# Down products of a feed-forward layer: two accumulations of 256 columns in one bank in place of one of 512

## The chip, the cores and the metric

The kernel runs on one core of one Trainium2 chip. The metric is the device time of one execution in microseconds; the median of three runs before the change is 2027.84 us (2025.33 to 2028.24). TensorE does the matrix products and reads its results out into accumulation banks of 512 float32 columns on 128 partitions; VectorE (DVE), ScalarE (ACT) and GpSimd (POOL) do the rest, SyncE (SP) starts most transfers.

## The reference, cut to what matters

The kernel computes one layer of a streaming encoder for 1152 tokens (1024 of a prompt and 8 x 16 of samples) and a model width of 1024: token mixing (a state-space half and a differential-attention half), cross-attention into 256 memory tokens, and a dense gated feed-forward network (FFN). The change touches only the last:

```python
hn = rms_norm(h, g_pre_ffn)
f = (jax.nn.silu(hn @ w_gate) * (hn @ w_up)) @ w_down     # hidden 2816
h = h + rms_norm(f, g_post_ffn)
```

All products are float32 in and out. The kernel splits each operand into a high part, rounded to the format that TensorE takes in one pass (fp32r), and a low part, the rest, and adds three products: high by high, high by low, low by high.

## The kernel before, in words

`three(out, pairs, release)` (lines 217 to 227) is the helper for every such product. For each pair of operands it issues three matmuls into one bank: line 222 (high, high), line 225 (high, low) and line 226 (low, high). The first of each matmul's operands is the stationary one (128 x 128, loaded by a weight load of its own ahead of every matmul, the PEld rows), the second is the moving one, whose columns are streamed. In the profile's rows the moving tile stands first: `bank<-w_hi,hid_h 128*128 128x512` moves 512 columns of w_hi past the stationary hid_h. `release` names pairs whose first matmul tells POOL that a weight slot has become free (semaphore w_used).

Weights come as items of 128 x 1024: SP loads them into w_raw, POOL splits each into w_hi and w_lo (`split`, lines 578 and 580), four slots of each. They are waited for with w_ready.

Where `three` is used, with the number of moving columns:

- token-major projections (`tm_chunk`), 256 columns of w past stationary NH/NL, 8 pairs (24 matmuls) to a bank; between them memory projections (`mem_unit`), 256 columns as well
- output projections (`join_unit`), 256 columns of w past stationary YH/NL, and later OH/OL, 24 matmuls to a bank
- scores of the cross-attention (`x_scores`), 256 columns of mkh/mkl past stationary QXh/QXl: two groups of 6 matmuls, one into each half of one bank
- linear projections (`lin_unit`) and the FFN's gate and up products (`up_unit`): 384 columns of the activations past stationary w, 24 matmuls to a bank
- the FFN's down products (`down_unit`): 512 columns of w past a stationary tile of the hidden, 2 pairs (6 matmuls) to a bank

The FFN goes through the hidden in 11 groups of 256. One group is 12 up units (288 matmuls), then SiLU on ACT, product, rounding and rest on DVE and ACT (`hid_raw`, `hid_high`, `hid_low`) into hid_h and hid_l, all of them two buffers; the down products of a group run after the up products of the next. A down is 18 units (9 token tiles x 2 column halves of the output), 108 matmuls. Unit q takes bank 6 + q % 2, waits until DVE has added what was in it (f_de) and, when its last matmul ends, gives f_dn; DVE's `add_down` (line 2053) adds the whole bank to ACC. On TensorE two groups are one pass of a hardware loop of 5 passes (`Fori`); the last down stands behind the loop, uses 6 banks, and is followed tile by tile by the final norm: ACT squares (line 244), DVE scales (`last_scale`, line 2059), POOL adds the residual, SP stores.

Of the kernel before, what the change touches and what calls it, by code (L numbers as in the profile page):

```python
# [65 lines left out]
def build(nc, x_in, mem_in, wall, wdt, consts, vecs, gains, rows, kc, vc, h0, sconv, cmk, cmv,  # L66
          y_o, k_o, v_o, ssm_o, conv_o, mk_o, mv_o, zs_d, q_d, h_d):
    with ExitStack() as ctx:
# [28 lines left out]
        whi, wlo = [T[f"w_hi{i}"] for i in range(4)], [T[f"w_lo{i}"] for i in range(4)]  # L97
# [71 lines left out]
        g = T.__getitem__  # L169
# [47 lines left out]
        def three(out, pairs, release=()):  # L217


            n = len(pairs)  # L220
            for i, (ah, al, bh, bl) in enumerate(pairs):
                m = mm(out, ah, bh, start=(i == 0), stop=False)  # L222
                if i in release:
                    m.then_inc(w_used, 1)
                mm(out, ah, bl, start=False, stop=False)  # L225
                m = mm(out, al, bh, start=False, stop=(i == n - 1))  # L226
            return m
# [5 lines left out]
        def tok(t):  # L233
            return slice(P * t, P * t + P)
# [380 lines left out]
        def _(pe):  # L615
# [50 lines left out]
            for kind in range(4):  # L666
                tm_chunk(kind, 0)
                tm_chunk(kind, 1)
                if kind == 2:
# [10 lines left out]
                    for t in range(NT):  # L680
                        m = nc.tensor.transpose(B[7][:, SH * t:SH * t + SH], g("dtr")[0:SH, tok(t)], ident[0:SH, 0:SH])
# [3 lines left out]
            with pe.Fori(0, KT // 4) as i:  # L685
                for s in range(4):
                    pe.wait_ge(w_ready, I_XB + s + 1 + 4 * i)
                    for c in range(CH):
# [4 lines left out]
                              release=((0,) if c == 0 else ())).then_inc(xb_mm, 1)  # L693
# [70 lines left out]
            for t in range(NT):  # L764
# [6 lines left out]
                for h in range(SH):  # L771
                    m = mm(B[6][:, SP_ * h:SP_ * h + SP_], g("MT")[:, h, :], g("xdt")[:, SP_ * h:SP_ * h + SP_],  # L772
                           start=True, stop=True)
# [4 lines left out]
                if t < NT - 1:  # L778
                    for gr in range(2):
                        m = mm(B[7][:, 256 * gr:256 * gr + 256], g("Btm")[:, gr, :], g("xdd")[:, 256 * gr:256 * gr + 256],  # L780
                               start=True, stop=True)
# [20 lines left out]
            for t in range(NT):  # L802
                if t < DB:
                    new_state(t)
                for w in range(2):
# [5 lines left out]
                    for h in range(H):  # L811
                        m = nc.tensor.transpose(B[6 + w][:, tok(h)], g(f"qkr{t % 2}")[:, w, tok(h)], ident)
# [91 lines left out]
            for u in range(U):  # L904
# [19 lines left out]
                if u == 17:  # L924
                    pe.wait_ge(a_yte, 3)
                    for h in range(H):
                        m = nc.tensor.transpose(B[7][:, tok(h)], g("oTs")[:, h, :], ident)
                    m.then_inc(b_sum, 1)
                if u == 18:
                    pe.wait_ge(b_p, DB + 1)  # L930
                    for h in range(H):
                        m = nc.tensor.transpose(B[7][:, tok(h)], g("QTs")[:, h, :], ident)
# [168 lines left out]
            def down(par, n0, s0, ready, hid):  # L1101
                pe.wait_ge(w_ready, ready)
                pe.wait_ge(f_hl, hid)
                for q in range(2 * NT):
                    pe.wait_ge(f_de, n0 + q + 1)
                    down_unit(par, s0, q, B[6 + q % 2],
                              ((0,) if q == 0 else (1,) if q == 2 * NT - 1 else ())).then_inc(f_dn, 1)

            def down_unit(par, s0, q, out, release=()):

                t, half = q // 2, slice(512 * (q % 2), 512 * (q % 2) + 512)
                return three(out, [(g(f"hid_h{par}{f}")[:, tok(t)], g(f"hid_l{par}{f}")[:, tok(t)],
                                    whi[(s0 + f) % 4][:, half], wlo[(s0 + f) % 4][:, half]) for f in range(2)], release)

            for n in range(WOVEN, 4 * NT):
                join_unit(pe, 1, I_WX, n, OH, OL)
# [20 lines left out]
            for q in range(2 * NT):  # L1137
                if q >= 6:
                    pe.wait_ge(f_de, 2 + last + q - 5)
                down_unit(0, 0, q, B[q % 6]).then_inc(f_dn, 1)  # L1140
# [1038 lines left out]
```

## Time and profile before

| | |
|---|---|
| median of 3 runs | 2027.84 us (2025.33 to 2028.24) |
| profiled execution, its own time | 2031.52 us |
| its span, first to last instruction | 2029.7 us |
| TensorE matmul busy (PE) | 1885.5 us, 93%, 12283 matmuls |
| TensorE weight load busy (PEld) | 1761.2 us, 87% |
| VectorE / ScalarE / GpSimd busy | 40% / 26% / 25% |
| mean granted TensorE clock | 0.955 |

The busy time of TensorE is the time in which some matmul is in flight; consecutive matmuls overlap, so a row's duration (0.39 us for 512 columns) is longer than what one costs in a stream. What one costs is the distance from its start to the start of the next. Starts are given to 0.01 us, so the distance is read from the first and the last of many.

### The profile page before, as it was taken

Reading aid. Unit: us, or ns where it says so; the run is one execution under the profiler, and the core shown is the slowest. Engines: PE = TensorE matmul, PEld = TensorE weight load, DVE = VectorE, ACT = ScalarE, POOL = GpSimd, SP = SyncE. Lnnn points to the kernel's source line nnn. Section 1 sums busy time; section 2 is a strip of 40 time slices with the busy share of each in tenths; the row PEclk is TensorE's granted clock in tenths of the full one; section 3 lists DMA queues with packets and bytes.
Section 4 is the critical chain, followed back from the end, with each engine's and each line's share of the span. In section 5 each row is a group of like instructions: output and inputs, shape, how many; then the busy total and the mean of one; then the engine's idle time right before and its main releaser. Section 6 shows DMA issues by size and latency. Waiting matters only on the chain.

```text
span 2029.7 us, 29875 instructions
## 1 busy us (share of the span) xinstructions
PE 1885.5 (93%) x12283; PEld 1761.2 (87%) x12283; DVE 816.2 (40%) x1633; ACT 523.1 (26%) x1279; POOL 508.0 (25%) x299
## 2 busy tenths in 40 slices
PE   7999999878677789989999999999999999999996
PEld 6999899767456669989988989999999999999995
DVE  5354116585665662361453361312322322322327
ACT  5200112265355663242343241010010010000002
POOL 3444442131000001212200312421421421421323
PEclk9999999997777889999999999999999999999998
DMA  5333331200530021121264321110110110110132
GB/s 211 111 117 111 103 133 43 101 27 21 194 106 8 1 93 64 70 108 52 84 229 153 112 99 42 53 52 21 55 48 21 62 41 21 62 41 21 62 124 93
DMA packets 56246, 160.99 MB, mean 79 GB/s; under 512 B 4176, under 2 KB 13904, under 8 KB 55888
## 3 DMA queue, kind: packets, MB, share of 16 engines
q1 hardware_dynamic: 35296, 117.13, 16.7%
q10 hardware_dynamic: 20848, 42.45, 5.9%
q8 instruction: 70, 1.15, 0.2%
q14 instruction: 32, 0.26, 0.0%
HBM read 131.41 MB, written 28.16 MB: 79 GB/s over the span
## 4 chain that ended last, share of the span: by engine, by line
PE 80%; DVE 10%; ACT 5%; issue 4%; DMA 1%; POOL 0%; ACTq 0%; SPq 0%; DVEq 0%; POOLq 0%
PE bank L222 23%; PE bank L225 23%; PE bank L226 23%; DVE at_sm L1830 1%; PE bank L995 1%; DVE H L347 1%; DVE ACC L2059 1%; PE bank L851 1%; PE bank L260 1%; PE bank L772 1%; DVE MT L1771 1%; DVE E L1764 1%; PE bank L744 1%; PE bank L840 1%; PE bank L893 1%
## 5 line engine op out<-in xcount | busy, mean ns | idle before, releaser
L578 POOL CAST w_hi<-w_raw 128x1024 fp32r<-128x1024 f32 x130 | 140.8, 1083 | 1371.2 <-PE bank L222 1205.5
L222 PE MATMUL bank<-OH,w_hi 128*128 128x384 f32 x1056 | 355.3, 336 | 0.0
L226 PE MATMUL bank<-OH,w_lo 128*128 128x384 f32 x1056 | 355.0, 336 | 0.0
L225 PE MATMUL bank<-OL,w_hi 128*128 128x384 f32 x1056 | 354.9, 336 | 0.0
L580 POOL TENSOR_TENSOR w_lo<-w_raw,w_hi 128x1024 fp32r<-128x1024 f32 x130 | 321.8, 2475 | 10.4
L226 PE MATMUL bank<-w_hi,NL 128*128 128x256 f32 x864 | 242.5, 281 | 0.0
L2039 DVE TENSOR_TENSOR hr<-sg,bank 128x384 f32<-128x384 f32 x66 | 36.5, 554 | 431.8 <-PE bank L226 431.8
L225 PEld LDWEIGHTS bank<-OL,w_hi 128*128 128x128 f32 x1056 | 198.6, 188 | 0.4
L222 PEld LDWEIGHTS bank<-OH,w_hi 128*128 128x128 f32 x1056 | 198.6, 188 | 0.4
L226 PEld LDWEIGHTS bank<-OH,w_lo 128*128 128x128 f32 x1056 | 198.6, 188 | 0.0
L2053 DVE TENSOR_TENSOR ACC<-ACC,bank 128x512 f32<-128x512 f32 x180 | 122.7, 685 | 109.5 <-PE bank L226 109.5
L226 PEld LDWEIGHTS bank<-w_hi,NL 128*128 128x128 f32 x864 | 164.6, 190 | 0.0
L222 PE MATMUL bank<-w_hi,NH 128*128 128x256 f32 x576 | 161.2, 280 | 0.0
L225 PE MATMUL bank<-w_lo,NH 128*128 128x256 f32 x576 | 160.2, 278 | 0.0
L225 PE MATMUL bank<-w_lo,hid_h 128*128 128x512 f32 x396 | 156.7, 396 | 0.0
L226 PE MATMUL bank<-w_hi,hid_l 128*128 128x512 f32 x396 | 156.7, 396 | 0.0
L222 PE MATMUL bank<-w_hi,hid_h 128*128 128x512 f32 x396 | 156.5, 395 | 0.0
L1604 ACT ACTIVATE sg<-bank 128x384 f32<-128x384 f32 x66 | 32.4, 490 | 416.8 <-PE bank L226 416.8
L225 PE MATMUL bank<-NL,w_hi 128*128 128x384 f32 x384 | 129.1, 336 | 0.0
L222 PEld LDWEIGHTS bank<-w_hi,NH 128*128 128x128 f32 x576 | 109.2, 190 | 0.0
L225 PEld LDWEIGHTS bank<-w_lo,NH 128*128 128x128 f32 x576 | 108.9, 189 | 0.0
L1613 ACT ACTIVATE hid_h<-hr 128x384 fp32r<-128x384 f32 x66 | 34.7, 525 | 278.8 <-DVE hr L2039 278.8
(343 smaller groups left out, 3722.2 us busy)
## 6 DMA issues: line engine op xcount, KB each, us to landing
w_raw<-in_wall SPq DMA_DIRECT2D x130, 512.0 KB, 3.3
scratch_h<-H ACTq DMA_DIRECT2D x6, 1536.0 KB, 5.3
MIX<-in_cmk SPq DMA_DIRECT2D x8, 1024.0 KB, 5.3
cV<-in_cmv SPq DMA_DIRECT2D x8, 1024.0 KB, 5.2
H<-in_x SPq DMA_DIRECT2D x1, 4608.0 KB, 17.4
H<-scratch_h SPq DMA_DIRECT2D x1, 4608.0 KB, 16.0
Hback<-scratch_h ACTq DMA_DIRECT2D x1, 4608.0 KB, 14.0
out_y<-Hback SPq DMA_DIRECT2D x9, 512.0 KB, 2.6
```

The lines of the kernel that those rows point to most:

```text
L222: m = mm(out, ah, bh, start=(i == 0), stop=False)
L225: mm(out, ah, bl, start=False, stop=False)
L226: m = mm(out, al, bh, start=False, stop=(i == n - 1))
L260: m = nc.tensor.transpose(turn_bank(z, j)[:, tok(i)], src[:, tok(4 * j + i)], ident)
L347: STT(out=res[:, t, :], in0=mix[:, t, :], scalar=col(S_V, n), in1=res[:, t, :], op0=ALU.mult, op1=ALU.add).then_inc(j_res, 1)
L578: pool.tensor_copy(whi[s][:], raw[s % 2][:]).then_inc(w_hi, 1)
L580: pool.tensor_tensor(wlo[s][:], raw[s % 2][:], whi[s][:].bitcast(F32), ALU.subtract).then_inc(w_ready, 1)
L744: m = mm(B[5][:, P * j + DS * b:P * j + DS * b + DS], g("h0t")[:, b, tok(j)], XC[:, 6 + j // 2, lo:lo + DS], start=True, stop=True)
L1604: act_f(g(f"sg{n % 2}")[:], B[2 * (n % 3)][:, 0:NC], ACT.Silu).then_inc(f_sg, 1)
L1613: act_f(g(f"hid_h{gi % 2}{f}")[:, cs(c)], g(f"hr{n % 2}")[:], ACT.Copy).then_inc(f_hh, 1)
L2039: TT(g(f"hr{n % 2}")[:], g(f"sg{n % 2}")[:], B[2 * (n % 3) + 1][:, 0:NC], ALU.mult).then_inc(f_hr, 1)
L2053: TT(a, a, bank_[:, :], ALU.add).then_inc(f_de, 1)
```

## The change

A down unit keeps its bank, its operands, its waits and its one signal f_dn. In place of 6 matmuls of 512 columns it issues two accumulation groups of 6 matmuls of 256 columns, the first into columns 0 to 255 of the bank, the second into 256 to 511, each with the two pairs. The weight-slot release moves to the second group. DVE still adds 512 columns at a time.

```diff
             def down_unit(par, s0, q, out, release=()):
 
-                t, half = q // 2, slice(512 * (q % 2), 512 * (q % 2) + 512)
-                return three(out, [(g(f"hid_h{par}{f}")[:, tok(t)], g(f"hid_l{par}{f}")[:, tok(t)],
-                                    whi[(s0 + f) % 4][:, half], wlo[(s0 + f) % 4][:, half]) for f in range(2)], release)
+                t = q // 2
+                for w0 in (0, 256):
+                    part = slice(512 * (q % 2) + w0, 512 * (q % 2) + w0 + 256)
+                    m = three(out[:, w0:w0 + 256],
+                              [(g(f"hid_h{par}{f}")[:, tok(t)], g(f"hid_l{par}{f}")[:, tok(t)],
+                                whi[(s0 + f) % 4][:, part], wlo[(s0 + f) % 4][:, part]) for f in range(2)],
+                              release if w0 else ())
+                return m
```

## Rows read from the trace of the kernel before

**Rows 1.** The page's part 1 and TensorE's lines of part 2 (40 slices, tenths).
```profile
PE 1885.5 (93%) x12283; PEld 1761.2 (87%) x12283; DVE 816.2 (40%) x1633; ACT 523.1 (26%) x1279; POOL 508.0 (25%) x299
PE   7999999878677789989999999999999999999996
PEclk9999999997777889999999999999999999999998
```

**Rows 2.** Page, part 4: shares of the chain that ended last, by engine.
```profile
PE 80%; DVE 10%; ACT 5%; issue 4%; DMA 1%; POOL 0%; ACTq 0%; SPq 0%; DVEq 0%; POOLq 0%
```

**Rows 3.** Groups by form, down matmuls: source line, engine, tiles, shape, count, busy us, mean ns.
```profile
L222 PE MATMUL bank<-w_hi,hid_h 128*128 128x512 f32 x396 | 156.5, 395 | 0.0
```

**Rows 4.** Timeline, TensorE, one down and its neighbours: start us, duration us, line, tiles.
```profile
1362.20 0.34 PE L226 MATMUL bank<-OH,w_lo 128*128 128x384 f32 x1
1362.38 0.39 PE L222 MATMUL bank<-w_hi,hid_h 128*128 128x512 f32 x1
...
1387.33 0.40 PE L226 MATMUL bank<-w_hi,hid_l 128*128 128x512 f32 x1
1387.57 0.34 PE L222 MATMUL bank<-OH,w_hi 128*128 128x384 f32 x1
...
1462.68 0.34 PE L222 MATMUL bank<-OH,w_hi 128*128 128x384 f32 x1
```

**Rows 5.** Timeline, TensorE, token-major projections: 168 matmuls, then 72.
```profile
138.25 0.28 PE L222 MATMUL bank<-w_hi,NH 128*128 128x256 f32 x1
...
157.29 0.28 PE L222 MATMUL bank<-w_hi,NH 128*128 128x256 f32 x1
...
165.78 0.28 PE L222 MATMUL bank<-w_hi,NH 128*128 128x256 f32 x1
```

**Rows 6.** Timeline, TensorE, first output projection, steady part: 638 matmuls.
```profile
779.77 0.28 PE L222 MATMUL bank<-w_hi,YH 128*128 128x256 f32 x1
...
854.92 0.29 PE L226 MATMUL bank<-w_hi,NL 128*128 128x256 f32 x1
```

**Rows 7.** Timeline, TensorE, cross-attention scores: 12 matmuls behind others, 10 after a pause.
```profile
936.05 0.34 PE L226 MATMUL bank<-YH,w_lo 128*128 128x384 f32 x1
936.23 0.29 PE L222 MATMUL bank<-mkh,QXh 128*128 128x256 f32 x1
...
937.67 0.33 PE L222 MATMUL bank<-YH,w_hi 128*128 128x384 f32 x1
...
1024.46 0.28 PE L225 MATMUL bank<-mkl,QXh 128*128 128x256 f32 x1
...
1025.64 0.28 PE L226 MATMUL bank<-mkh,QXl 128*128 128x256 f32 x1
```

**Rows 8.** Busy time by stretch: stretch, length, PE, PEld, DVE, ACT, POOL (instructions), clock, DMA.
```profile
218.00:283.00 65.00, 65.00 (x575) 65.00 (x575) 4.33 (x13) 12.43 (x28) 27.33 (x17) 1.00 0.23 76
1312.50:1362.20 49.70, 49.70 (x289) 49.70 (x287) 6.26 (x11) 5.57 (x11) 17.15 (x10) 1.00 0.13 43
1363.00:1387.00 24.00, 24.00 (x104) 19.32 (x104) 12.28 (x19) 0.53 (x1) 3.53 (x2) 1.00 0.13 44
```

**Rows 9.** Timeline, VectorE in the same down; in brackets the idle time before and its releaser.
```profile
1366.77 0.69 DVE L2053 TENSOR_TENSOR ACC<-ACC,bank 128x512 f32<-128x512 f32 x1 [0.71 <-PE bank L226]
1368.17 0.69 DVE L2053 TENSOR_TENSOR ACC<-ACC,bank 128x512 f32<-128x512 f32 x1 [0.71 <-PE bank L226]
```

**Rows 10.** Timeline, GpSimd around the same down.
```profile
1362.90 1.04 POOL L578 CAST w_hi<-w_raw 128x1024 fp32r<-128x1024 f32 x1 [0.69 <-PE bank L222]
1364.02 2.59 POOL L580 TENSOR_TENSOR w_lo<-w_raw,w_hi 128x1024 fp32r<-128x1024 f32 x1
1387.40 1.04 POOL L578 CAST w_hi<-w_raw 128x1024 fp32r<-128x1024 f32 x1 [20.78 <-PE bank L222]
1388.52 2.40 POOL L580 TENSOR_TENSOR w_lo<-w_raw,w_hi 128x1024 fp32r<-128x1024 f32 x1
```

**Rows 11.** Chain that ended last, in order of time, around the last down: start us, us, what.
```profile
1991.22 0.25 PE bank L226
1991.50 0.70 DVE ACC L2053
1992.28 1.15 ACT jk L244 x2
1993.45 1.28 ACT L245
...
2025.10 1.23 DVE Hback L2081
```

## The prediction

> **What bounds the kernel now.** I read the page's busy shares and slices first: TensorE is busy 93% of the span, and from the slice at about 1200 us to the last but one it stands at nine tenths in every slice, at the full clock [rows 1]. The shares of the chain that ended last say the same from the other side: 80% of it is TensorE, 10% DVE [rows 2]. So in the FFN, where the change lies, the question is what one matmul costs in a stream, and nothing else unless something begins to make TensorE wait. The groups by form give 396 matmuls of each of the three kinds of down matmul and a mean of 395 ns [rows 3], but that is a length in a pipeline, not a cost. The timeline gives the cost: from the first matmul of one down to the first up matmul behind it 1387.57 - 1362.38 = 25.19 us for 108 matmuls, 233.3 ns each, and the following down ends at 1462.68, 75.11 us later, for 288 up and 108 down matmuls; 75.11 - 25.19 = 49.92 us is 173.3 ns for each up matmul of 384 columns, so there is no gap anywhere in a period, the loop's jump back included [rows 4]. The stretches confirm it: PE is busy 49.70 of 49.70 us and 24.00 of 24.00 us, clock 1.00, that is the upper of the two levels, 2.4 GHz [rows 8].
>
> **What the change removes and adds.** It removes 6 matmuls of 512 columns and 6 weight loads in each of 11 x 18 units, and adds 12 matmuls of 256 columns and 12 weight loads. The columns streamed are the same. What decides is whether two matmuls of 256 cost more or less than one of 512, 466.7 ns for two and 233.3 for one. I count in threes, because `three` issues threes: one triple of 512 costs 700.0 ns (3 x 233.3, rows 4), and two triples of 256 take its place.
>
> How many of them set the end: 10 downs in the loop hold 10 x 18 x 2 = 360 triples. Of the last down only the start counts. The chain in order of time leaves TensorE at 1991.22 with the second unit and from there runs through DVE and ACT to the end, 2025.10 + 1.23 us [rows 11]; so two units, 4 triples, make 364.
>
> The trace has the new matmul (256 moving columns, fp32r, a new stationary tile each time, clock 1.00) in several stages, and it does not have one price there:
>
> - 168 matmuls of the token-major projections take 157.29 - 138.25 = 19.04 us, 113.3 ns each, 340.0 ns a triple [rows 5]
> - the next 72 of the same line, the same shape and the same stage take 165.78 - 157.29 = 8.49 us, 117.9 ns each, 353.8 a triple [rows 5]
> - 638 matmuls of the output projection take 75.15 us, 117.8 each, 353.4 a triple [rows 6]
> - the scores, which have the new code's very form (two groups of 6, one in each half of a bank, entered from a stream of 384), take 1.44 us for 12, 120.0 each, 360.0 a triple; another ten of them take 1.18 us, 118.0 each, 354.0 a triple [rows 7]
>
> Half of 700.0 is 350.0 ns, so the break-even of 116.7 ns a matmul lies between the levels. In terms of the kernel:
>
> - at 340.0: 2 x 340.0 - 700.0 = -20 ns, x 364 = -7.3 us
> - at 353.4: 2 x 353.4 - 700.0 = +6.8 ns, x 364 = +2.5 us
> - at 360.0: +20 ns, x 364 = +7.3 us
>
> These are the two ends and the middle. I take the middle one. The reason to stay away from the low end: the operands and the shape do not fix the level, since rows 5 hold both levels in one stage, and the level then lasts for whole units; the low level stands only in the token-major stage, while each later stage of 256 columns is at 117.8 to 120.0. The reason not to take the high end although the scores have the nearest form: they show 118.0 as well as 120.0, and their moving tiles are other ones, whereas the long streams that move w, as the down does, stand at 113.3 or 117.8. What I think limits a matmul of 256 is the weight load in front of it: in the stretch of 256 columns the weight-load side is busy 65.00 of 65.00 us, in the down only 19.32 of 24.00 [rows 8]. (That alone proves nothing: it is busy 49.70 of 49.70 us beside 384 columns too, which show one price everywhere.) With 512 columns a load has 233 ns to hide in and with 256 about 117, so the gain of a shorter matmul is there only if the load just fits.
>
> The Trainium skill, "TensorE: Matmul & The Clock Gate", section "Back-to-back issue gap", has a rule that speaks against the change: a warm matmul costs its columns at 2.4 GHz plus a fixed 2.5 ns, so each matmul more costs 2.5 ns. By that, an estimate from that page, 1092 more matmuls would add 2.7 us; rows 4 don't agree with its 215.8 ns for 512 columns, they have 233.3, and rows 5 have 113.3 where it gives 109.2. It would leave the forecast where it is.
>
> **What lies beside.** DVE adds a bank in 0.69 us and then waits 0.71 us for TensorE [rows 9]; a unit becomes 12 x 117.8 = 1.41 us instead of 1.40 (1.36 or 1.44 at the ends), so the wait f_de still finds the bank free, two units back. Nothing is added on DVE. No wait is added on TensorE; queued behind it would be only its own matmuls. The release moves: in unit 0 by six matmuls of 256, 6 x 117.8 = 0.71 us later, so the cast at 1362.90 and the rest until 1366.61 end at about 1367.3; that item is first needed by the next up at 1387.57, 20 us later. In the last unit the release comes three matmuls before the end as before, now 0.35 us before it instead of 0.70. The cast at 1387.40 starts 0.35 us later and its rest ends at 1391.3 instead of 1390.92 [rows 10]; the up unit that reads this slot is the third, 2 x 24 x 173.3 ns = 8.3 us behind 1387.57. Both cost nothing; were that cover gone, it would be 0.35 us a period, 3.5 us in all. SP's loads follow POOL's splits by the same 0.35 to 0.71 us. The loop's body holds more instructions, at a rate (a load and a matmul every 113 to 118 ns) that rows 5 and 6 show TensorE being fed without a gap, though outside a loop.
>
> **The sum.** The profiled execution took 2031.52 us, 1.82 more than its span, and 3.68 more than the median of the runs. 2031.52 + 2.5 = 2034.0 for such an execution, and against the median 2027.84 + 2.5 = 2030.3 us. I count below 0.2%, 4.1 us, as no change: about what a measurement of this kernel can tell.
>
> **Rivals.**
>
> The load just fits (faster). The down falls into the state of most of rows 5, 340.0 ns a triple: -7.3 us, 2020.5 us. For it: the down's 512-column triples come in a steady stream without a pause, they move w as rows 5 do, and a unit entered from the 384-column stream has its loads well ahead. Against it: the scores are entered from such a stream too and are not at this level [rows 7]. Chance 0.33.
>
> The load does not fit (slower). Each short group of 6 behaves like the scores at 936.23, 120.0 ns from the first matmul on [rows 7]: +7.3 us, 2035.1 us. It decides as soon as the mean is over 118.6 ns: 4.1 us over 2184 matmuls of 256 is 1.9 ns above 116.7. For it: the same form of code, two groups and two halves of a bank, with the boundary between the groups included in the 1.44 us. Against it: the 118.0 of the later scores and all the streams that move w. Chance 0.29, which takes in 0.03 for a pause at the loop's jump now that the body is longer, of which no row shows a price.
>
> The change does not do what it says: none that I see, since each half has its own first and last matmul and DVE reads the bank after the last.
>
> Forecast, 117.8 ns or a mixture of levels from down to down: chance 0.38.
>
> **How the numbers follow.** Faster by over 0.2% is the first rival, 0.33; slower by over 0.2% is the second, 0.29; within 0.2% is the forecast, 0.38. Cases of both signs hold most of the chance, so the range must reach to both ends: 2027.84 - 7.3 and + 7.3, and some 0.7 us for the scatter of the medians: 2019.8 to 2035.8. The forecast's own range is 2027.5 to 2032, mixtures taken in.
>
> **What would show it.** Between the first down matmul and the next up matmul, 216 matmuls of 256: 25.4 us by the forecast, 24.5 if the load fits, 25.9 if it doesn't, against 25.19. The up products should stay at 49.9 us a period, DVE's wait before an add at about 0.7 us, and the tail from TensorE's last link to the end at its 35 us. A down with a level that changes within it would give a mixture. The prediction would be wrong in kind if TensorE idled at the start of a down or of an up, or if the period changed outside the down.

## The result and the profile after the change

The changed kernel takes 2042.6 us, median of 4 runs (2039.7 to 2046.48), against 2027.26 us of 4 runs of the kernel before on the same chip (2025.33 to 2028.24). The ratio is 1.0070, 95% interval 1.0056 to 1.0084: slower by 0.7%, some 14 us. The forecast was 2030.3 us, no change; the time lies outside the range (2019.8 to 2035.8). The rival on the slower side had the sign, but neither the size nor, as will be seen, the cause.

The profiled execution of the changed kernel took 2041.20 us, its span is 2039.3 us. The page's busy shares and slices, and the instruction queue's line (packets, MB, share), which for the kernel before reads 70 packets, 1.15 MB, 0.2%:

```profile
PE 1881.9 (92%) x13471; PEld 1807.8 (89%) x13471; DVE 818.1 (40%) x1633; ACT 523.0 (26%) x1279; POOL 509.1 (25%) x299
...
PEclk9999999997776989999999999999999999999998
...
q8 instruction: 113, 1.85, 0.4%
```

TensorE is busy for 3.6 us less than before and the span is 9.6 us longer [rows 1]: the loss isn't in the price of a matmul, it is for the most part idle time. The weight loads are busy for 46.6 us more, since there are more of them, DVE and POOL for 1 to 2 us more; what stands out is the transfer of instructions, 113 packets in place of 70. The waits of TensorE in the FFN (tile, line <- what ended them: total us, times, longest) name two kinds, and the kernel before has none there:

```profile
PE bank L222 <- issue: 7.9, 4, 2.2
PE bank L222 <- DVE ACC L2058: 2.1, 9, 0.2
PE bank L222 <- DVE ACC L2056: 0.2, 1, 0.2
```

**The four waits for nothing.** "issue" is time for which the profile shows no releaser. The timeline of TensorE puts the four at the jump of the loop, between the last down matmul of a pass and the first up matmul of the next, of which there are four in five passes:

```profile
1384.93 0.28 PE L226 MATMUL bank<-w_hi,hid_l 128*128 128x256 f32 x1
1387.40 0.44 PE L222 MATMUL bank<-OH,w_hi 128*128 128x384 f32 x1 [2.19 <-issue]
1387.68 0.34 PE L225 MATMUL bank<-OL,w_hi 128*128 128x384 f32 x1
```

From start to start it is 2.47 us where 0.12 us would be the matmul's own cost. And behind two of the four the clock falls; it isn't the length of the pause that decides, since these two idled for 1.95 and 1.88 us and the other two for 2.19 and 1.91. The stretches (columns as in rows 8): the pause itself, then 3.9 us behind another jump at the mean clock 0.57, that is for the most part at the lower of the two levels, 1.2 GHz; then the same length behind a jump where it stays up. Thirteen matmuls where the other has 23:

```profile
1384.93:1387.40 2.47, 0.28 (x3) 0.08 (x2) 0.69 (x1) 0.00 (x0) 2.21 (x2) 1.00 0.00 0
1692.75:1696.68 3.93, 3.93 (x13) 3.93 (x14) 0.00 (x0) 0.00 (x0) 3.85 (x3) 0.57 0.33 117
1539.64:1543.60 3.96, 3.96 (x23) 3.96 (x24) 0.00 (x0) 0.00 (x0) 3.88 (x3) 1.00 0.33 98
```

**The ten waits for DVE.** They stand at the third unit of each of the ten downs of the loop (the last down, with its six banks, has none by this view). The timeline of one down, all engines:

```profile
1437.43 0.28 PE L222 MATMUL bank<-w_hi,hid_h 128*128 128x256 f32 x1
...
1438.55 1.04 POOL L578 CAST w_hi<-w_raw 128x1024 fp32r<-128x1024 f32 x1 [1.29 <-PE bank L222]
...
1438.83 1.17 DVE L2049 TENSOR_TENSOR hid_l<-hr,hid_h 128x384 fp32r<-128x384 f32 x1 [0.59 <-ACT hid_h L1618]
...
1439.92 1.27 DVE L2058 TENSOR_TENSOR ACC<-ACC,bank 128x512 f32<-128x512 f32 x2
...
1440.13 0.28 PE L226 MATMUL bank<-w_hi,hid_l 128*128 128x256 f32 x1
...
1440.65 0.39 PE L222 MATMUL bank<-w_hi,hid_h 128*128 128x256 f32 x1 [0.23 <-DVE ACC L2058]
1440.88 0.28 PE L225 MATMUL bank<-w_lo,hid_h 128*128 128x256 f32 x1
```

TensorE's 24 matmuls of the first two units are through at 1440.13 + 0.12, and unit 2 starts at 1440.65: 0.52 us from start to start, 0.40 more than a matmul's own (the wait that the view counts, 0.23, is shorter, since the matmul before is still in flight for part of it), and the matmul behind it comes another 0.11 us late, 0.23 us after it in place of 0.12: some 0.5 us a down. It needs the bank that DVE's first add empties (the row of 1.27 us holds two adds of 0.68 us, so the first ends at 1440.60), and that add is late because the subtraction ahead of it on DVE, hid_low, takes 1.17 us. In the kernel before, the subtraction of a down takes 0.57 us, and the first add, of 0.67 us, follows at once:

```profile
1363.78 0.57 DVE L2044 TENSOR_TENSOR hid_l<-hr,hid_h 128x384 fp32r<-128x384 f32 x1 [0.59 <-ACT hid_h L1613]
...
1364.28 0.67 DVE L2053 TENSOR_TENSOR ACC<-ACC,bank 128x512 f32<-128x512 f32 x1
```

The difference is POOL's cast. Before, it starts 0.52 us into the down (1362.90 - 1362.38, rows 4 and 10) and the subtraction starts 1.40 us into it, when the cast is nearly done; after, the cast starts 1.12 us into the down, and the subtraction runs beside it. The cast has moved because the change has moved the release of unit 0 into the second half.

**Where 12.8 us went.** I take the FFN from its first down matmul to the end of the span: 2029.7 - 1287.26 = 742.44 us before, 2039.3 - 1284.07 = 755.23 us after, 12.8 us more. (What stands ahead of it, which the change doesn't touch, was 3.2 us shorter in this execution, which leaves the 9.6 us of the span.) By parts, each against 25.19 us a down and 49.93 us the ups of a group:

| part of the FFN | after | difference |
|---|---|---|
| 5 downs in the middle of the body | 25.11 us each | -0.4 us |
| 4 downs ahead of the jump, pause included | 28.29, 27.18, 28.04, 27.16 us | +9.9 us |
| the 12 up units behind each of the 4 jumps | 50.03, 50.03, 51.60, 51.59 us | +3.5 us |
| from the tenth down, with the last one right behind it, to the end | 66.14 us | -0.3 us |

With the pauses left out, eight of the ten downs of the loop cost nothing: 24 matmuls at 117.8 ns, the 0.5 us at unit 2, then the rest at 113.3 to 113.4 ns. The other two, both ahead of a jump, stay at 117.8 ns behind the wait and take 25.9 us, 0.7 more than before. Both stretches of the down above, and the whole down:

```profile
1437.43:1440.65 3.22, 2.99 (x25) 2.78 (x24) 2.37 (x4) 0.53 (x1) 2.02 (x2) 1.00 0.44 163
1440.65:1462.54 21.89, 21.89 (x193) 21.89 (x193) 10.85 (x16) 0.00 (x0) 1.60 (x1) 1.00 0.07 25
1437.43:1462.54 25.11, 24.88 (x218) 24.67 (x217) 13.23 (x19) 0.53 (x1) 3.62 (x2) 1.00 0.12 43
```

The tail stands: TensorE's last link at 2001.04, and 34.97 us to the end of the last row of the chain, against 35.1 [rows 11].

```profile
2001.04 0.13 PE bank L226
2001.19 0.70 DVE ACC L2058
...
2034.78 1.23 DVE Hback L2086
```

### The profile page after: what moved, and what is told of

The parts are those of the page before. It is cut to its first block, busy times and chain, and to the rows that moved or that the text cites. A ratio compares the mean times of both kernels' runs of the same rounds, so it can differ in the third digit from the quotient of the medians.

```text
span 2039.3 us, 32251 instructions
## 1 busy us (share of the span) xinstructions
PE 1881.9 (92%) x13471; PEld 1807.8 (89%) x13471; DVE 818.1 (40%) x1633; ACT 523.0 (26%) x1279; POOL 509.1 (25%) x299
## 4 chain that ended last, share of the span: by engine, by line
PE 78%; DVE 12%; ACT 5%; issue 4%; DMA 1%; POOL 0%; ACTq 0%; DVEq 0%; SPq 0%; POOLq 0%
PE bank L222 23%; PE bank L226 23%; PE bank L225 23%; DVE at_sm L1835 1%; DVE H L347 1%; PE bank L995 1%; DVE ACC L2064 1%; PE bank L851 1%; PE bank L260 1%; DVE E L1769 1%; DVE ACC L2058 1%; DVE MT L1776 1%; PE bank L772 1%; PE bank L744 1%; PE bank L840 1%
## 5 line engine op out<-in xcount | busy, mean ns | idle before, releaser
L222 PE MATMUL bank<-w_hi,hid_h 128*128 128x256 f32 x792 | 220.9, 279 | 2.4 <-DVE ACC L2058 2.1
L226 PE MATMUL bank<-w_hi,hid_l 128*128 128x256 f32 x792 | 219.8, 278 | 0.0
L225 PE MATMUL bank<-w_lo,hid_h 128*128 128x256 f32 x792 | 219.8, 278 | 0.0
L222 PEld LDWEIGHTS bank<-w_hi,hid_h 128*128 128x128 f32 x792 | 149.3, 188 | 4.4 <-DVE ACC L2058 3.9
L226 PEld LDWEIGHTS bank<-w_hi,hid_l 128*128 128x128 f32 x792 | 149.0, 188 | 0.0
L225 PEld LDWEIGHTS bank<-w_lo,hid_h 128*128 128x128 f32 x792 | 148.7, 188 | 0.0
```

## The experiments

My theory after reading this profile had two parts. A: the loop's body has grown past what TensorE can jump back to without fetching it anew, and the late release is a second, smaller loss. B, its rival for the pause: the pace; 256-column matmuls ask for instructions faster than they come, and the jump, where fetching starts over, shows it first. The size of the body is counted from the program: 792 matmuls before, 1008 after, each with its weight load, and some 60 others, 1646 and 2078 instructions; the traces have 1645 and 2078 records of TensorE between two jumps.

### The two causes taken apart

**early_release**: the changed kernel, with the release of unit 0 back in its first half.

```diff
-                              release if w0 else ())
+                              release if (w0 == 0) == (q == 0) else ())
```

> The changed kernel, but unit 0 of a down releases its weight slot in its first half, as before the change. Theory: the late release let POOL's cast run into DVE's hid_low (1.17 us in place of 0.57), and the first add came so late that TensorE waited at unit 2 (0.4 to 0.5 us, 11 times). So here hid_low is 0.57 us again and there is no gap at unit 2; the pauses at the loop's jump (4 of about 2 us) stay. The matmuls ran at 117.8 ns before that wait and mostly at 113.3 behind it; if the wait itself sets the level, all 216 stay at 117.8, 25.44 us a down in place of 25.11, and the time is 2043 to 2046 us; if they go to 113.3 without it, 2036. Rival: the wait comes from the halves themselves (the bank is filled in two groups), and then it stays, with hid_low at 0.57.

Measured 2041.56 us (4 runs, 2039.46 to 2045.27), ratio to the kernel before 1.0067 (1.0046 to 1.0088). The wait at the third unit is gone, the subtraction is back at 0.56 us beside a cast that starts 0.42 us into the down:

```profile
1435.17 0.28 PE L222 MATMUL bank<-w_hi,hid_h 128*128 128x256 f32 x1
...
1435.59 1.04 POOL L578 CAST w_hi<-w_raw 128x1024 fp32r<-128x1024 f32 x1 [0.58 <-PE bank L222]
...
1436.58 0.56 DVE L2049 TENSOR_TENSOR hid_l<-hr,hid_h 128x384 fp32r<-128x384 f32 x1 [0.60 <-ACT hid_h L1618]
...
1460.61 0.34 PE L222 MATMUL bank<-OH,w_hi 128*128 128x384 f32 x1
```

Yet the down is longer than with the wait, 1460.61 - 1435.17 = 25.44 us against 25.11: all 216 matmuls now run at 117.8 ns, in all eleven downs. The wait had been followed by the low level, and what the mend gave back the level took. The pauses at the jump stay, and are all that TensorE waits for in the FFN:

```profile
PE bank L222 <- issue: 7.8, 4, 2.2
```

**unrolled**: the changed kernel with the five passes written out.

```diff
-            with pe.Fori(0, (NG - 1) // 2) as i:
+            for i in range((NG - 1) // 2):
```

> The changed kernel with the FFN's hardware loop on TensorE written out in full (5 passes, no jump). Theory: the body with 216 more matmuls and as many weight loads no longer stays in the instruction store and has to be fetched again at each jump back: 4 pauses of about 2 us (7.9 us of idle in all) and, behind two of them, the lower clock for about 4 us (1.8 us each). Without a jump these go: 2042.6 - 7.9 - 3.6 = 2031 us, and the waits at unit 2 stay. Rival: the pause is a wait for weights or for the adds at the start of the next group; then it stays at 4 places of about 2 us and the time is 2042.

Measured 2031.45 us (10 runs, 2023.51 to 2033.47), ratio 1.0002 (0.9989 to 1.0016). No pause is left, the ten waits for DVE remain:

```profile
PE bank L222 <- DVE ACC L2058: 2.1, 9, 0.2
PE bank L222 <- DVE ACC L2056: 0.2, 1, 0.2
```

Behind them six of the ten downs are at the low level (25.11 us) and four at 117.8 ns (25.94 us). Without the jump the change is what the forecast had called it, no change; so the whole loss that can be measured hangs on the jump.

**unrolled_early**: both edits.

> Both together: written out in full, and the early release. Then only the price of a matmul of 256 is left, as the forecast took it: by the 117.8 level everywhere 2027.3 + 2.5 = 2030 us, by the 113.3 level 2020, by 120.0 2034.6. If the wait at unit 2 is what moves the stream to the lower level, it is 2030 and every down takes 25.44 us.

Measured 2032.6 us (10 runs, 2027.91 to 2037.58), ratio 1.0013 (1.0000 to 1.0025), +2.6 us. TensorE waits for nothing in the FFN. A down in its stretch:

```profile
1366.18:1391.62 25.44, 25.44 (x217) 25.44 (x217) 12.70 (x19) 0.53 (x1) 3.73 (x2) 1.00 0.13 43
```

216 matmuls of 117.8 ns: this kernel does what the forecast priced. By the profile a down costs 0.25 us more, 2.5 us in ten, as the forecast said; the measured 2.6 us agree, with an interval from 0 to 5.1.

**before_unrolled**: the kernel before, written out in the same way. It tells whether writing out is itself worth something.

> The kernel before with the loop on TensorE written out in full. Control for the written-out kernels: before, nothing paused at the jump, so this should be the same, 2027 us within 2, with more bytes fetched by the instruction queue (1.70 MB or so in place of 1.15). If it is faster or slower, the written-out kernels have to be compared with this one.

Measured 2028.82 us (10 runs, 2023.46 to 2031.31), ratio 0.9996 (0.9985 to 1.0007): nothing. The loop costs nothing as long as its body is short.

**before_late_release**: the kernel before, whole, with only the release of unit 0 moved to its second pair, three matmuls of 512 later.

```diff
-                              ((0,) if q == 0 else (1,) if q == 2 * NT - 1 else ())).then_inc(f_dn, 1)
+                              ((1,) if q in (0, 2 * NT - 1) else ())).then_inc(f_dn, 1)
```

> The kernel before (512 columns), with one edit: unit 0 of a down releases its weight slot with its second pair, 3 matmuls or 0.70 us later, as late as in the changed kernel. Theory: POOL's cast then starts about 1.2 us into the down in place of 0.52, DVE's hid_low takes 1.17 us in place of 0.57 and TensorE waits about 0.4 us at unit 2: some 10 x 0.4 to 0.5 = 4 to 5 us, 2031.5 us. Rival: without the halves nothing waits, 2027.3.

Measured 2034.58 us (10 runs, 2030.15 to 2038.67), ratio 1.0024 (1.0012 to 1.0035), +4.9 us. The second cause alone, at 512 columns, and with its mechanism in the timeline:

```profile
1440.74 1.04 POOL L578 CAST w_hi<-w_raw 128x1024 fp32r<-128x1024 f32 x1 [1.39 <-PE bank L222]
...
1440.92 1.27 DVE L2044 TENSOR_TENSOR hid_l<-hr,hid_h 128x384 fp32r<-128x384 f32 x1 [0.59 <-ACT hid_h L1613]
...
1442.84 0.50 PE L222 MATMUL bank<-w_hi,hid_h 128*128 128x512 f32 x1 [0.37 <-DVE ACC L2053]
```

Its ten waits are 3.8 us in the view of waits:

```profile
PE bank L222 <- DVE ACC L2053: 3.4, 9, 0.4
PE bank L222 <- DVE ACC L2051: 0.4, 1, 0.4
```

From start to start they are more. This down takes 1465.35 - 1439.52 = 25.83 us against 25.19, 0.64 us more, and so do the other nine: 6.4 us by the profile, where 4.9 (2.4 to 7.1) are measured.

```profile
1439.52 0.39 PE L222 MATMUL bank<-w_hi,hid_h 128*128 128x512 f32 x1
...
1465.35 0.34 PE L222 MATMUL bank<-OH,w_hi 128*128 128x384 f32 x1
```

Here nothing pays them back, since matmuls of 512 stay at 233.3 ns behind the wait.

### Size of the body or pace

The next kernels halve only some units. All have the early release, and all are the changed kernel with this edit and another condition:

```diff
+            def HALVES(par, q):
+                return par == 1
...
-                t = q // 2
-                for w0 in (0, 256):
-                    part = slice(512 * (q % 2) + w0, 512 * (q % 2) + w0 + 256)
-                    m = three(out[:, w0:w0 + 256],
+                t, W = q // 2, 256 if HALVES(par, q) else 512
+                for w0 in range(0, 512, W):
+                    part = slice(512 * (q % 2) + w0, 512 * (q % 2) + w0 + W)
+                    m = three(out[:, w0:w0 + W],
...
-                              release if w0 else ())
+                              release if W == 512 or (w0 == 0) == (q == 0) else ())
```

**one_down_halved**: as shown, the down ahead of the jump halved, the other of 512; 900 matmuls in the body.

> Halves only in the second down of the loop's body (18 of its 36 units), the other and the last down as before, release as before. The body then holds about 1646 + 18 x 12 = 1862 instructions of TensorE (matmuls, weight loads and the rest), as against 2078 in the changed kernel and 1646 before. Theory: it stays resident, no pause at the jump, the instruction queue at 1.15 MB; 5 downs at 117.8 ns cost 25.44 - 25.19 = 0.25 us each: 2027.3 + 1.3 = 2028.5. Rival: any halved down ahead of the jump brings the pause (it is the quicker issue of small matmuls that outruns the fetch, not the size of the body): 4 pauses of 2.2 us and the clock, 2037.

Ratio 1.0062 (1.0041 to 1.0084), from three runs with a median of 2044.07 us. The pauses are there, 7.7 us in four. The expectation had this body jump back freely; that size was wrong.

**body_30_units** and **body_34_units**: `par == 1 or q >= 6` and `par == 1 or q >= 2`.

> Halves in 30 of the 36 units of the loop's body: about 2006 instructions, 128,400 bytes at 64 each. Theory of a store of 2048 instructions: no pause at the jump, instruction queue at 1.15 MB. If the store needs some room to read ahead, this one pauses as well. Rival, pace and not size: it pauses.

> Halves in 34 of the 36 units: about 2054 instructions. Theory of a store of 2048: 4 pauses of about 2.2 us at the jump, idle 7.8 us, the instruction queue at some 1.8 MB. Should this one not pause, the limit lies between 2054 and 2078, or it is another thing that counts.

One run each: 2037.78 and 2042.93 us, beside a median of 2028.76. Four pauses in both, 8.3 and 7.7 us. They don't tell size from pace either. Both expectations went by a limit of 2048 instructions, and body_30_units, with 2006, should then have had no pause; so the limit, if it is one of size, lies lower. What else they gave is the level of the streams, below.

**first_down_halved**: `par == 0`, so that 512-column matmuls stand ahead of the jump, with the same 900 matmuls in the body.

> Halves only in the first down of the loop's body (and in the last down, behind the loop). The body has the same 1862 instructions as with the second down halved, but ahead of the jump stand 108 matmuls of 512 columns at 233.3 ns. If the size of the body decides, the 4 pauses of about 2.2 us stay and the instruction queue is at 1.75 MB or more; if the pace ahead of the jump decides (small matmuls outrun the fetch), they go and the queue is at 1.2 MB.

One run, 2036.64 us, beside 2030.45. The timeline of TensorE at a jump:

```profile
1380.91 0.40 PE L226 MATMUL bank<-w_hi,hid_l 128*128 128x512 f32 x1
1383.46 0.44 PE L222 MATMUL bank<-OH,w_hi 128*128 128x384 f32 x1 [2.16 <-issue]
```

Twenty-five microseconds of 512-column matmuls, at half the rate of instructions, do not let the fetching get ahead: four pauses of 2.2 us at most, 8.0 us in all. That speaks against the pace, but the body still holds halved units.

**long_body_512**: the kernel before, not one down halved, with a body of four groups instead of two in two passes, the other two groups behind it; 1584 matmuls in the body.

```diff
-            with pe.Fori(0, (NG - 1) // 2) as i:
-                for x in range(2):
+            with pe.Fori(0, 2) as i:
+                for x in range(4):
...
+            for x in range(2):
+                group(x, 4)
```

> The kernel before, all downs at 512 columns, but the loop holds four groups in its body and is passed twice, with the last two groups written out behind it. No matmul of 256 columns stands in the FFN. The body has twice the 1646 instructions. If the size of the body is what counts, its one jump back costs a pause of about 2.2 us (and perhaps the lower clock behind it), and packets of the instruction queue flow through the whole loop, as in the changed kernel (42 between 1300 and 1940 us as against 3 before). If it takes matmuls of 256 columns to bring the pause, there is none.

One run, 2025.08 us, beside one of the kernel before at 2022.62. There is one jump and one pause, with no 256-column matmul in the whole FFN:

```profile
1528.96 0.39 PE L226 MATMUL bank<-w_hi,hid_l 128*128 128x512 f32 x1
1531.23 0.44 PE L222 MATMUL bank<-OH,w_hi 128*128 128x384 f32 x1 [1.88 <-issue]
```

With this rival B falls: a pause at the jump comes without any 256-column matmul. What these bodies share is their length.

**body_12_units**, **body_6_units**, **body_4_units**, **body_2_units**: `par == 1 and q >= 6`, `12`, `14` and `16`, to find the length.

> Halves in the last 12 units of the second down: 1790 instructions, 7.0 pieces. By size it brackets the limit further: pauses if it lies below 1790. By pace: a pause.

> Halves in the last 6 units of the second down: 1646 + 72 = 1718 instructions, 6.7 pieces of the 16 KB in which the instruction queue moves them (1.15 MB in 70 packets). By size: the limit lies between 1646 and 1862, and this one tells which side of 1718 it is on; no pause and 1.15 MB if it still fits. By pace: 36 matmul pairs of 256 just ahead of the jump, so a pause, perhaps a shorter one.

> Halves in the last 4 units: 1694 instructions. Same two outcomes; with the run before it, it places the limit within 24 instructions.

> Halves in the last 2 units of the second down: 1646 + 24 = 1670 instructions. Known so far: 1646 stays resident, 1718 does not. Either it pauses at the 4 jumps (about 2.2 us each) with some 37 instruction packets in the loop, or it has no pause and 3 packets.

| halved units in the body | matmuls (instructions, as counted) | pauses at the jump | one run, us | beside, us |
|---|---|---|---|---|
| 0 (before) | 792 (1646) | none | | |
| 2 | 804 (1670) | none | 2030.95 | 2022.62 (one run) |
| 4 | 816 (1694) | none | 2027.78 | 2022.62 (one run) |
| 6 | 828 (1718) | 9.3 us, 4 times | 2046.67 | 2030.45 |
| 12 | 864 (1790) | 7.9 us, 4 times | 2034.88 | 2030.45 |
| 18 (one_down_halved) | 900 (1862) | 7.7 us, 4 times | | |
| 36 (changed) | 1008 (2078) | 7.9 us, 4 times | | |

It is a step, not a slope: between 816 and 828 matmuls in the body the whole pause appears. The single times are worth little here (the kernel before alone reads from 2022.62 to 2034.56 us over these comparisons), the waits are what tells. The instruction queue's line in the stretch from 1300 to 1940 us says what the pause is. The kernel before:

```profile
q8 instruction: 3, 0.05, 0.0%
```

The kernel with four halved units:

```profile
q8 instruction: 3, 0.05, 0.0%
```

The kernel with six:

```profile
q8 instruction: 38, 0.62, 0.4%
```

The changed kernel, and the same written out:

```profile
q8 instruction: 42, 0.69, 0.4%
```

```profile
q8 instruction: 34, 0.56, 0.4%
```

Up to four units the three packets fall into the first pass, and from 1372 us on the loop runs on what is already there; from six on its code comes again, 16 KB a packet, nine or ten packets a pass. Written out, nearly as many packets come and nobody waits, so the transfer as such isn't the cost. The packets' own times in the changed kernel's trace show what is: at each of the four jumps one starts 0.15 to 0.65 us before the pass's last down matmul (at 1384.78 us for the one shown above), takes about 1 us, and the first up matmul starts 2.6 to 2.9 us behind the packet's start. That fits a fetch which can begin only when the jump is reached.

### The level of a stream, and a version that uses it

**unrolled_512_first**: in the kernels above a stream of 256 columns entered from up products (384) always ran at 117.8 ns, one entered from at least 36 matmuls of 512 mostly at 113.4 (body_30_units 4 of 5 such downs of the loop, body_12_units 5 of 5; after only 12 matmuls of 512, in body_34_units, 2 of 5). (The shorter streams of body_6_units, run beside this test, and of body_2_units and body_4_units, run after it, do not agree among themselves: 4 of 5, 5 of 5 and none of 5.) So: all downs begin with six units of 512 columns and go on with twelve halved, in the written-out form with the early release.

```diff
+            def HALVES(par, q):
+                return q >= 6
```

> Written out in full, early release, and in each of the 11 downs the first 6 units at 512 columns and the other 12 in halves. In the kernel with 30 halved units, the 256-column stream that was entered from 512 columns ran at 113.4 ns in 5 of 6 cases, and the one entered from 384 columns at 117.8 in all. If the way of entry sets the level, every down is 12 x 4 x 10 ns = 0.48 us shorter than with 512 columns: 10 x 0.48 = 4.8 us, 2023 us against 2028, 0.24% faster. If the level is drawn anew each time, some downs lie at 117.8 (+0.16 us each) and the gain is 1 to 4 us.

Measured 2025.44 us (7 runs, 2022.38 to 2030.88) against 2030.45 (11 runs), ratio 0.9976 (0.9964 to 0.9989): 0.24% faster than the kernel before, and the only one of these kernels that is faster beyond its interval. Ten of the eleven downs take the low level. Two downs, one of each kind:

```profile
1365.25:1390.61 25.36, 25.36 (x181) 23.71 (x181) 12.73 (x19) 0.53 (x1) 3.64 (x2) 1.00 0.12 42
1440.54:1465.28 24.74, 24.74 (x181) 23.06 (x181) 12.73 (x19) 0.53 (x1) 3.63 (x2) 1.00 0.13 43
```

24.74 us against 25.19 is 0.45 us a down. Nine of the ten downs of the loop have it, the tenth costs 0.17: 3.9 us, and 5.0 us is measured (2.2 to 7.3).

## Why the prediction was wrong

**The price of a stream: right.** "at 353.4: +2.5 us" is what unrolled_early costs, +2.6 us (0 to 5.1), every down at 117.8 ns. That the operands and the shape don't fix the level was right too; the changed kernel has both levels in each down, and its downs in mid-body come out at 25.11 us, 0.3 us under the forecast's 25.4, wait included. That is luck: the late release costs 0.5 us there, and the low level behind it, which the forecast didn't have, gives back more. The weight load as the reason was argued there and has not been tested.

**The scores' level (120.0 ns), the slower rival: wrong cause.** No down of any kernel ran at it.

**"The loop's body holds more instructions, at a rate ... fed without a gap": the step that failed.** It asked about a rate and took rows 5 and 6, straight code, as the answer. The question was whether the body is still there when the loop jumps back, and the sign that rows 4 show no gap at the jump holds only for the body they were taken from. Worse, the pause was given 0.03 and no size. It costs 7.9 us of idle time in four pauses (8.6 us from start to start, a matmul's own taken off), and behind a pause the clock may fall: 1.7 us more behind two of the four. These 12 us are most of the 9.9 and 3.5 us of the table; the rest is the two downs ahead of a jump that ran at 117.8 ns, 0.7 us each. The Trainium skill, "Runtime: NRT & Kernel Launch", section "Instruction fetch mechanics", has the mechanism: TensorE's instruction memory is 128 KiB or 2048 instructions, filled in blocks of 16 KiB, and a taken branch whose target isn't in the current window of two blocks must fetch it first and stalls. The runs agree in kind, with pauses of 1.7 to 2.5 us at the jump and packets of 16 KB. They differ in size on both sides: by my count 1718 instructions already stall, under the 2048, while by the window of two blocks the kernel before would stall as well, and a body of 1694 instructions jumps back without a packet.

**"Both cost nothing": the second failure, on the release.** The check went to who needs the slot, 20 us later, and that was right. What was missed is what the moved work runs beside. POOL's cast, 0.6 us later, falls on DVE's hid_low and doubles it (0.57 to 1.17 us, and 1.27 in before_late_release), and the first add, behind it in DVE's order, is what TensorE's unit 2 waits for. That alone is worth +4.9 us (2.4 to 7.1) at 512 columns; the step had priced 0.35 us a period. In the changed kernel the 113.3 ns behind the wait pay it back in eight of ten downs, so early_release gains nothing that can be measured. The Trainium skill, "SBUF — State Buffer", section "Who interferes with whom", says that a DVE instruction with two inputs in SBUF contends with a GpSimd instruction that reads SBUF; the trace agrees: beside the cast the subtraction takes 1.17 us in place of 0.57, while the cast keeps its 1.04.

**"the wait f_de still finds the bank free": wrong for the same reason.** It was worked out from the steady adds of rows 9, not from the first add of a down, which stands behind hid_low.

**The ups and the tail: right but for the clock.** Ups that don't follow a jump and the tail of 35 us are unchanged.

## What to carry to other kernels

An edit that adds instructions to a loop's body has a price that no row of the steady state shows: count the body before and after, and look at the instruction queue in the loop's stretch, where three or four packets in the whole loop meant that it was resident, and nine or ten a pass that every jump paused. When a signal moves, follow the released work to the engine that it will run beside, not only to the one that needs it. And where a matmul has two prices in one trace, measure both; here the cheap one came in 10 of 11 downs with six units of 512 columns in front of the stream.

## What the hardware showed that was not expected

- The jump: free up to 816 matmuls in the body, 1.7 to 2.5 us a time from 828, and not growing with the length from there (7.7 to 9.3 us in four, up to 1008). Whether something in the place of the code in memory moves the limit was not tried.
- The clock: behind such a pause it fell in 14 of 33 cases (two of four in the changed kernel, one of four in early_release, three of four in body_12_units), behind pauses of 1.8 to 2.3 us, and stayed up behind others of 1.7 to 2.5. 384-column triples then took 960 ns in place of 520 over some 4 us. Matmuls of the changed kernel there, timeline of TensorE:

```profile
1693.81 0.53 PE L225 MATMUL bank<-OL,w_hi 128*128 128x384 f32 x1
1694.13 0.53 PE L226 MATMUL bank<-OH,w_lo 128*128 128x384 f32 x1
```

- The level of a 256-column stream: set when it is entered and kept for the whole of it. Entered from 384 columns it was 117.8 ns in every down, from 36 or more matmuls of 512 columns 113.4 in 30 of 38, behind a wait either. The starts in the traces, taken to the nanosecond, part the 38: ahead of the entry the 512-column matmuls come either evenly, 233 or 234 ns apart, or in turn 231 and 236 ns apart. Entered evenly (22 streams) or right behind a distance of 235 or 236 ns (8) the stream had the low level; entered right behind one of 231 ns (8, the five of body_4_units among them) it had the high one. Behind only 12 matmuls of 512 this does not hold. Streams of 384 and 512 columns have one mean price, 173.3 and 233.3 ns. What in TensorE makes the level is open; no run here isolates it.
